# Short products of a hybrid decoder step spread into wide projection blocks, with S5 outputs, loads and copies reordered

## The reference

```
proj = rmsnorm(x) @ w_in                  # 1024 -> z 1024, xBC 1536, dt 16, u 1024
xBC  = silu(causal_conv4(xBC)); dt = softplus(dt + bias)
y    = ssd(x, dt, A, B, C, D, h0)         # 16 heads of 64, state 128, chunks of 128 tokens
y_ssd = rmsnorm(y * silu(z))
h    = scan(h = a*h + b*u)                # S5: 64 groups of 16 channels, complex state 64
s    = gelu(Re(c*h) + d*u);  y_s5 = rmsnorm(s * sigmoid(s @ w_glu + b_glu))
x   += concat(y_ssd, y_s5) @ w_out
x   += hier_moe(rmsnorm(x))               # 32 experts in 4 groups, 2 for each token
return rmsnorm(x), new conv, SSD and S5 states
```

## Time and profile before

| | |
|---|---|
| median of 3 runs | 1067.53 us (1066.47 to 1075.4) |
| the profiled execution, as a run | 1061.96 us |
| its span in the profile | 1059.7 us |
| its mean granted TensorE clock | 0.986 of full speed |
| busy: TensorE, VectorE, ScalarE, GpSimd | 961.3, 434.8, 331.1, 268.0 us |
| chain that ended last | PE 68%, DMA 23%, DVE 5% |
| its largest parts | wide blocks (L653) 24%, w_up loads 20%, L1023 9% |

### The profile page before, as it was taken

The page is one execution under the profiler, slowest core; times in us unless marked ns, Lnnn a source line. Parts: engine busy times, 40 slices in busy tenths (PEclk is TensorE's granted clock), DMA queues, the critical chain, the costliest instruction groups (busy, mean ns, idle before and its releaser), DMA issues.

```text
span 1059.7 us, 17219 instructions
## 1 busy us (share of the span) xinstructions
PE 961.3 (91%) x6496; PEld 682.0 (64%) x6497; DVE 434.8 (41%) x743; ACT 331.1 (31%) x662; POOL 268.0 (25%) x510
## 2 busy tenths in 40 slices
PE   6999999999999999999999999999877788998881
PEld 5889779877776788998765555555443444554440
DVE  6999877454466898951521111111100101111112
ACT  3025323453325784322422222232212121222113
POOL 1000888888421010000012222222222112222110
PEclk9999999999999999999999999999999999999996
DMA  7585172110098744255589999999999999999994
GB/s 268 125 142 92 29 121 81 41 63 22 12 223 226 254 147 175 87 238 239 218 323 392 396 383 398 385 394 397 395 396 395 396 413 404 409 410 408 425 385 167
DMA packets 73566, 277.54 MB, mean 262 GB/s; under 512 B 36953, under 2 KB 38873, under 8 KB 56497
## 3 DMA queue, kind: packets, MB, share of 16 engines
q1 hardware_dynamic: 63020, 252.67, 65.0%
q0 software_dynamic: 8720, 19.86, 6.8%
q10 hardware_dynamic: 1780, 4.41, 1.1%
HBM read 260.17 MB, written 25.61 MB: 270 GB/s over the span
## 4 chain that ended last, share of the span: by engine, by line
PE 68%; DMA 23%; DVE 5%; issue 2%; ACT 1%; POOL 0%; SPq 0%; ACTq 0%; POOLq 0%; DVEq 0%
PE ps L653 24%; DMA sb_arena<-w_up 20%; PE ps L1023 9%; PE ps L1037 7%; PE ps L1016 7%; PE ps L919 7%; PE ps L992 2%; DMA sb_arena<-ssm_in 2%; PE ps L685 1%; PE ps L741 1%; PE ps L798 1%; DVE sb_arena L1960 1%; PE ps L772 1%; PE ps L895 1%; PE ps L1030 1%
## 5 line engine op out<-in xcount | busy, mean ns | idle before, releaser
L653 PE MATMUL ps<-sb_arena 128*128 128x264 f32 (+1 forms) x1152 | 266.9, 392 | 9.1 <-DMA sb_arena<-wi 9.1
L653 PEld LDWEIGHTS ps<-sb_arena 128*128 128x128 f32 x1152 | 218.8, 191 | 57.5 <-DMA sb_arena<-wi 9.6
L1956 DVE TENSOR_TENSOR sb_s5b<-sb_s5b,ps 128x256 f32<-128x256 f32 x36 | 22.2, 617 | 408.0 <-PE ps L1023 408.0
L1023 PE MATMUL ps<-sb_arena 128*64 128x256 f32 x1152 | 131.3, 380 | 22.0 <-DMA sb_arena<-w_up 22.0
L1037 PE MATMUL ps<-sb_arena 128*64 128x512 f32 x576 | 131.5, 598 | 20.7 <-DVE sb_arena L1960 20.7
L1016 PE MATMUL ps<-sb_arena 128*64 128x256 f32 x1152 | 132.6, 383 | 16.5 <-DMA sb_arena<-w_gate 15.8
L1016 PEld LDWEIGHTS ps<-sb_arena 128*64 128x64 f32 x1152 | 83.6, 138 | 76.3 <-DMA sb_arena<-w_gate 27.0
L1023 PEld LDWEIGHTS ps<-sb_arena 128*64 128x64 f32 x1152 | 82.5, 137 | 67.1 <-DMA sb_arena<-w_up 28.9
L1388 ACT ACTIVATE sb_kxf<-ps,sb_gate_of 64x512 f32<-64x512 f32 x36 | 24.6, 683 | 301.1 <-PE ps L1037 301.1
L1037 PEld LDWEIGHTS ps<-sb_arena 128*64 128x64 f32 x576 | 39.0, 136 | 90.1 <-issue 60.9
L1415 DVE TENSOR_TENSOR sb_arena<-sb_arena 128x64 f32<-128x64 f32 (+12 forms) x86 | 78.0, 907 | 19.5 <-DMA sb_arena<-ssm_in 12.2
(11 more groups left out here) (308 smaller groups left out, 1210.3 us busy)
## 6 DMA issues: line engine op xcount, KB each, us to landing
sb_arena<-w_gate SPq DMA_DIRECT2D x32, 2048.0 KB, 33.7
sb_arena<-w_up SPq DMA_DIRECT2D x32, 2048.0 KB, 35.9
sb_arena<-w_down SPq DMA_DIRECT2D x32, 2048.0 KB, 35.6
sb_arena<-wi SPq DMA_DIRECT2D x28, 512.0 KB, 4.0
sb_arena<-w_out SPq DMA_DIRECT2D x4, 2048.0 KB, 8.5
sb_arena<-ssm_in POOLq DMA_DIRECT2D x8, 512.0 KB, 8.9
sb_arena<-wglu SPq DMA_DIRECT2D x8, 512.0 KB, 5.0
o_ssm_s<-sb_arena POOLq DMA_DIRECT2D x8, 512.0 KB, 4.0
```

The source lines that it names most:

```text
L653: last = mm(ps[:, b0 + h, 0:t1 - t0], ring[w % 3][:, k, :], src[:, k, t0:t1], start=k == 0, stop=k == KD - 1)
L1023: last = mm(ps[64 * r:64 * r + 64, 1, 0:256], xt[:, k, :], Wu[s][:, k, 256 * r:256 * r + 256], start=k == 0, stop=k == KD - 1)
L1956: V.tensor_tensor(hh.rearrange("p (j c) -> p c j", j=2), sg.rearrange("p (c j) -> p c j", j=2), ps[:, 1, 0:256].rearrange("p (c j) -> p c ...
```

## The change

Eight places are edited; what is computed stays the same.

1. SyncE issues ring loads 26 and 27 ahead of `y_store(0)`, and only 28 behind it.
2. GpSimd signals `h_done` once after the chunk recurrence and once more after the sample part; its own DMAs wait for both.
3. TensorE: Toeplitz rounds 8 to 15 stand one in each k step of block 17, the decay sums in the first five k steps of block 18, the sample steps two in each k step of block 19.
4. Chunk 4's y products stand in the k steps of block 30, its states behind that block.
5. Block 25 moves from ahead of the S5 outputs to behind their second half, so that both halves follow `ssd_y_off(2)` with only `ssd_c(2)` between.
6. ScalarE empties block 18 and runs the SiLU of convolution 8 ahead of the Exp of dE.
7. The GELU writes its output in order and reads its input at a stride; before, it read in order and wrote at a stride.
8. VectorE runs convolution 9 ahead of the wait for the decay sums.

```diff
--- before.py
+++ after.py
@@ -439,9 +439,10 @@
+            ring_load(26)
+            ring_load(27)
             y_store(0)
-            for w in range(26, 29):
-                ring_load(w)
+            ring_load(28)
...
@@ -559,13 +560,14 @@
+            pl.sem_inc(h_done, 1)
...
             nc.gpsimd.tensor_tensor(sst[:], sst[:], smp, ALU.add).then_inc(h_done, 1)
-            pl.wait_ge(h_done, 1)
+            pl.wait_ge(h_done, 2)
...
@@ -647,8 +649,16 @@
+                    if w == 17:
+                        toeplitz_round(8 + k)
+                    if w == 18 and k < 5:
+                        decay_sums(k)
+                    if w == 19:
+                        sample_steps(2 * k)
                     if w == 28:
                         pe.wait_ge(gelu_done, k + 1)
+                    if w == 30:
+                        ssd_y(4, k)
                     for h, (t0, t1) in enumerate(HALVES):
                         last = mm(ps[:, b0 + h, 0:t1 - t0], ring[w % 3][:, k, :], src[:, k, t0:t1],
...
@@ -732,8 +742,8 @@
-            pe.wait_ge(t_ld, 16 * 32)
-            for rd in range(16):
+            def toeplitz_round(rd):
+
                 if rd >= 2:
                     pe.wait_ge(lc_ev, rd - 1)
                 for q in range(4):
...
                               start=True, stop=True)
                 last.then_inc(lc_mm, 1)
 
-            pe.wait_ge(dt_done, 1)
-            pe.wait_ge(dt_ev, 2)
-            pe.wait_ge(bcs_ev, 1)
-            for c, (t0, n) in enumerate(CH):
+            def decay_sums(c):
+
+                n = CH[c][1]
+                if c == 0:
+                    pe.wait_ge(dt_done, 1)
+                    pe.wait_ge(dt_ev, 2)
+                    pe.wait_ge(bcs_ev, 1)
...
                 last = mm(ps[:, 7, 32 * c + 16:32 * c + 32], ones[0:n, :], dav[0:n, c, :], start=True, stop=True)
-            last.then_inc(cs_mm, 1)
+                if c == 4:
+                    last.then_inc(cs_mm, 1)
+            def sample_steps(first):
+
+                for h in range(first, first + 2):
...
+                if first == HEADS - 2:
+                    last.then_inc(ds_mm, 1)
+
+            pe.wait_ge(t_ld, 16 * 32)
+            for rd in range(8):
+                toeplitz_round(rd)
             for w in range(17, 20):
                 wide(w)
-            for h in range(HEADS):
...
-            last.then_inc(ds_mm, 1)
...
@@ -806,26 +827,37 @@
-            def ssd_c(c):
+            def ssd_y(c, i):
-                pe.wait_ge(sa_evd, c + 1)
-                if c:
-                    pe.wait_ge(yo_ev, 2 * c)
-                for i in range(8):
-                    if i % 4 == 0:
-                        pe.wait_ge(m_done, 2 * c + 1 + i // 4)
-                    for r in range(2):
...
-                last.then_inc(y_mm, 1)
+                if i == 0:
+                    pe.wait_ge(sa_evd, c + 1)
+                    if c:
+                        pe.wait_ge(yo_ev, 2 * c)
+                if i % 4 == 0:
+                    pe.wait_ge(m_done, 2 * c + 1 + i // 4)
+                for r in range(2):
...
+                if i == 7:
+                    last.then_inc(y_mm, 1)
+
+            def ssd_states(c):
                 pe.wait_ge(sa_eva, c + 1)
                 for g in range(2):
                     last = mm(ps[:, 6 + g, :], btok[0:n, g, :], xde[0:n, 8 * g:8 * g + 8, :], start=True, stop=True)
...
+
+            def ssd_c(c):
+
+                for i in range(8):
+                    ssd_y(c, i)
+                ssd_states(c)
...
@@ -848,11 +880,11 @@
             ssd_a(2)
             ssd_b(2)
             ssd_y_off(2)
-            wide(25)
             pe.wait_ge(yo_ev, 4)
             state_outputs(0, 8)
             ssd_c(2)
             state_outputs(8, 8)
+            wide(25)
             ssd_a(3)
...
@@ -867,8 +899,9 @@
             wide(28)
             pe.wait_ge(yo_ev, 8)
             wide(29)
-            ssd_c(4)
-            for w in range(30, 36):
+            wide(30)
+            ssd_states(4)
+            for w in range(31, 36):
                 wide(w)
...
@@ -1183,11 +1216,12 @@
             conv_silu(7)
             ac.wait_ge(dt_done, 1)
             decays(0)
+            raw_evac(8 + 10)
+            conv_silu(8)
             ac.wait_ge(de_in, 2)
             act_(dE, dE, ACT.Exp).then_inc(de_out, 1)
-            for i in range(10, XBC):
-                raw_evac(8 + i)
-                conv_silu(i - 2)
+            raw_evac(8 + 11)
+            conv_silu(9)
...
@@ -1237,8 +1271,8 @@
-                act_(yg[:, i, 0:NP_].rearrange("p (m j) -> p j m", j=J),
-                     yraw[:, i, 0:NP_].rearrange("p (j m) -> p j m", j=J), ACT.Gelu_apprx_tanh)
+                act_(yg[:, i, 0:NP_].rearrange("p (m j) -> p m j", j=J),
+                     yraw[:, i, 0:NP_].rearrange("p (j m) -> p m j", j=J), ACT.Gelu_apprx_tanh)
...
@@ -1623,13 +1657,14 @@
             link(V.memset(dE, 0.0))
+            conv(9)
             dv.wait_ge(cs_mm, 1)
...
-            for i in range(9, XBC):
+            for i in range(10, XBC):
                 conv(i)
```

19 lines of the change are left out of this document (10 added, 9 removed).

## The result

The changed kernel takes 1085.18 us (median of four runs, 1084.94 to 1085.44), the one before in the same comparison 1067.0 us (1065.36 to 1075.4): ratio 1.0154, 95% interval 1.0101 to 1.0208, or 18 us slower. The prediction was 1086.5 us in a range of 1076 to 1096. The sign, the size and the largest single term held. The sum held less well than it looks. Its own yardstick was the profiled execution of before, and against that the profiled execution of the changed kernel is 23.0 us longer (span 1082.7 against 1059.7), where the sum said 19. The other 5 us are in the kernel before, whose ordinary runs lie above its profiled one; the changed kernel's don't (its profiled execution is the run of 1084.94 us). That the two errors nearly cancel is luck. More on this at the experiment `mix`.

A forecast was written before the change was run, and what follows sets the result against it. TensorE was taken to bound the part up to 404 us and the DMA engines the expert part. Terms 4.1 + 3.1 - 1.2 - 0.7 + 2.3 + 6.4 + 5.1 gave +19 us on 1067.5: 1086.5 us, range 1076 to 1096.

The forecast's parts named there:

- largest single term: Ahead of block 31: its weight load, queued behind the wait for chunk 4's states, is no longer covered, +6.4 us.
- Toeplitz and decay sums: Blocks 17 and 18: spread short passes save a little waiting for weight loads, -0.5 us; lower bound -3.2.
- block 19 to `ssd_b(0)`'s third product: Narrow groups spread in block 19 (+3.3) and a second ScalarE table load (+1.3) delay the third product, +4.6 us.
- outputs ahead of block 25, waits: S5 outputs: the first and third rounds wait for VectorE, which block 25 had covered, +3.1 us.
- waits at block 26 and `ssd_a(4)`: Earlier loads 26 and 27 end block 26's wait, and VectorE is in time for `ssd_a(4)`, -1.2 us.
- GELUs, to the end of block 29: The GELUs' wait for the y load goes, each GELU stays at 1.15 us, -0.7 us; lower bound -2.0.
- chunk 4 in block 30: Eight groups of 16-row tiles spread in block 30 cost more than one run, +2.3 us; lower bound 0.
- block 31's weights: Block 31 waits for the weight load that SyncE issues behind its wait for chunk 4's states, +6.4 us.
- clock: TensorE's clock falls to half behind stands at ssd_b(0), the outputs and block 31, +5.1 us; bounds 0 and 8.5.
- Rival (b): Weight loads are hidden wherever short and wide products alternate: +9 us in all, 1077 us; chance 0.05.
- I add the difference to the median: Whole kernel: the sum in profiled-execution time, +19 us, is added to the median of 1067.5 us.
- (c): Faster: wide products among short ones spare clock falls of ordinary runs, 1.7 us each, fifteen needed for 1056; chance 0.03.

The follow-up runs named there:

- mix: Changed kernel with chunk 4, block 25, sample steps, ScalarE's order and GELU access put back, loads 31 to 33 ahead of their wait: 1062.5 us, ratio 0.9938.
- steps_run: Changed kernel with the 16 sample steps put back behind block 19 in one run: 1082.69 us.
- act_back: Changed kernel with ScalarE's order put back, the Exp of dE ahead of the copy of block 18: 1083.79 us.
- steps_act: Changed kernel with both the sample steps in one run behind block 19 and ScalarE's order put back: 1080.31 us.
- b25_after2: Changed kernel with block 25 between the second and the third S5 output round: 1077.56 us.
- ld31: Changed kernel with ring loads 31 to 33 ahead of SyncE's wait for st_ev 5 and the o_ssm_p store: 1081.60 us.

## Why the prediction was right, and where not

By the prediction's own steps, in the profiled executions (all counted on TensorE):

| step | predicted us | measured us |
|---|---|---|
| Toeplitz and decay sums | -0.5 | +0.1 |
| block 19 to `ssd_b(0)`'s third product | +4.6 | +4.7 |
| outputs ahead of block 25, waits | +3.1 | +2.9 |
| waits at block 26 and `ssd_a(4)` | -1.2 | -1.5 |
| GELUs, to the end of block 29 | -0.7 | +0.4 |
| chunk 4 in block 30 | +2.3 | +2.2 |
| block 31's weights | +6.4 | +6.6 |
| clock | +5.1 | +7.1 |
| sum | +19 | +22.5 |

- **Toeplitz rounds.** From the first of the spread rounds (179.15 us) to the end of block 17 (193.57) it takes 14.4 us, where 14.0 was expected and under 13.4 would have meant hidden loads; the two end when they ended before. The 0.05 us for each group came and went again on the way back: a group of eight short passes takes 0.85 us where a run takes 0.90, and the four wide passes behind it 0.95 where a block has 0.90. TensorE's timeline of the changed kernel:

```profile
182.79 1.01 PE L751 MATMUL ps<-sb_arena 128*128 128x75 f32 x8
183.64 1.11 PE L663 MATMUL ps<-sb_arena 128*128 128x264 f32 x4
184.59 1.01 PE L751 MATMUL ps<-sb_arena 128*128 128x75 f32 x8
```

  Rival (b), hidden weight loads, fell here. The Trainium skill's rule that the queue pulls weight loads ahead of running products where the row groups don't conflict or the background weights are the target (TensorE: Matmul & The Clock Gate, Step-by-step) bears on this. The trace agrees where a full-size tile follows a wide product: the weight load of the short group at 182.79 starts at 182.56, 0.23 us ahead of its product. It disagrees for the narrow tiles: 1.32 us for a k step of block 19 where 0.90 of wide passes and 0.13 of narrow ones would do.
- **Block 19.** 10.5 us was predicted and is measured; two table loads stand behind it; TensorE stands 2.9 us there (3 predicted). `steps_run`, `act_back` and `steps_act` confirm the two parts and that they add up at that product. The 0.08 us "to fill the pipe again" in the sum has no row behind it; in the changed kernel 0.22 us lie between the start of a narrow group and the next wide product (203.33 and 203.55), 0.09 over the 0.13 of its passes.
- **Outputs.** 0.95 us and 1.96 us (1.0 and 2.1 predicted), confirmed by `b25_after2`, which takes away the second only.
- **The wait at `ssd_a(4)`.** It went, but not as argued. "Comes 1.5 us earlier on the clock" does not follow from the prediction's own terms: 4.1 + 3.1 less block 25's 7.2 is 0. The last output round ends 5.8 us later than before (at 312.0, before at 306.2), and the wait goes because TensorE comes to `ssd_a(4)` 11.6 us later, not 6.
- **Chunk 4 and block 31.** Block 30 takes 11.55 us (11.6), the stand is 6.63 us, from the adds at 381.50 to block 31 at 388.09 (6.4 predicted). But the sentence on VectorE's sample work, "TensorE is by then later by about as much, so I add nothing", was right only because TensorE stood at block 31 first: `ld31` shows 2.3 us of it as soon as the load is in time.
- **GELU.** The wrong step is "One side stays strided, so I take 1.15". The duration did stay 1.15; what counts in a row of them is the step to the next, 1.02 before and 1.15 after. So where -0.7 was expected, block 28, which waits for the GELUs in either kernel, ends later. That `y_off(4)` now runs at full speed (1.89 us for 3.58 in the earlier trace rows) gives nothing, as predicted: behind it TensorE stands 0.88 us for the first GELU.
- **Clock.** This term was mis-sized and wrongly placed. I took 1.7 us for the stands in `ssd_b(0)`, 0.9 for those at the outputs and 2.5 ahead of block 31. Measured: no fall at `ssd_b(0)` in spite of its 2.9 us of standing (the clock is 1.00 from 213 to 221 us), 5.4 at the outputs, 1.7 behind block 31. The length of a fall was the error: I read 3.4 us from the earlier trace rows as the length of one, but at the outputs it goes on for 13.7 us. The cause given for the one at block 31 is not shown either. It begins at 381.3 us, while TensorE still works on the states (busy 0.40 of the 0.40 us from 381.00 to 381.40, at a mean clock of 0.93), just ahead of the stand, and `ld31` has it at the same place with no stand. That 7.1 us came where 5.1 was forecast, with one of the three falls missing and one six times as large as its term, is partly luck.
- **The median.** The step "I add the difference to the median" covered the short sum: the median of before has some 5 us that its profiled execution has not, and the changed kernel does not have them either. With 22.5 for the sum the same method would have said 1090, and been 5 too high. The rival of the other side, (c), looked for this in the clock alone; `mix` shows a gain of 5.8 us over the kernel before in ordinary runs, which the mean clock does not account for.

## What to carry to other kernels

Ahead of moving a block, ask what it covered: here a wide block covered two VectorE instructions, a weight load and a ScalarE chain, and each came out at the length that the trace of before shows from release to landing. When one stall is mended, look for the next chain that the same move made late; the first had hidden it. Spreading the short products among wide ones won nothing here (+0.1 us for 64 passes and the decay sums), and tiles narrower than the array cost 0.28 us a group more; but a wide block placed behind the first two rounds of short products took the stand away, and with it the fall of the clock, in both kernels that had it, where short products behind a stand of 1.8 us lost the clock in all nine. And when a part measured alone comes out at its forecast, look at the clock in both profiles before taking it as shown: falls that came and went between them were worth 1.7 to 3.4 us.
